# A two-block model kernel on one core: memory loaded ahead of x at the begin, and four k's of the second merge set into the stick-breaking attention

## The chip, the cores and the metric

One core of a Trainium2 chip runs one program. Its engines work side by side and meet through semaphores: TensorE (PE; its weight loads are listed as PEld), VectorE (DVE), ScalarE (ACT), GpSimd (POOL) and SyncE (SP), which issues most of the transfers. The metric is the program's time on the device in microseconds; less is better.

## The reference, cut to what matters

The model takes x (1024 positions by 1024) and a memory of 256 rows by 1024, all in float32. The first block computes

```
h   = rms_norm(x, norm_mix);  p = h @ w_in              # incl. the lora columns wd, ad, gd
x   = x + merged(rwkv7(p), conv(p)) @ w_out_mix
mem_n = rms_norm(mem, norm_mem);  k, v = split(mem_n @ w_kv)
x   = x + cross_attention(rms_norm(x, norm_xattn), k, v) @ w_xo
x   = x + relu(rms_norm(x, norm_mlp) @ w_up)^2 @ w_down
```

and the second block, on the normed result,

```
y_a = gated_delta_rule(...) @ w_up_a;   y_b = stick_breaking(q_b, k_b, v_b) * silu(z_b) @ w_up_b
out = x + (gates_a * y_a + gates_b * y_b) @ w_out
```

Stick-breaking weighs key j for query i by sigmoid(z_ij) times the product of (1 - sigmoid(z)) over the keys between j and i.

## The kernel before, in words

Every matrix product is made to float32 precision from parts: an operand is rounded to fp32r (hi), what is left is a second part (lo), and three products hi-hi, lo-hi, hi-lo are summed. So each weight tile is loaded raw, rounded (w_hi) and subtracted (w_lo) before TensorE can use it. `Weights` (L89) does this for streams of tiles with two or three slots; GpSimd rounds and subtracts in `split_tile` (L155), or ScalarE in `round_tile` and another engine in `subtract_tile`.

The program is a chain of blocks. At the end of a block all engines meet; each engine's order inside a block is written out by hand. The next block's first loads and splits are already issued inside the block (`following`).

**The begin** (`start_to_loras`, L4493). SP loads two tiles of memory and eight tiles of x (128 rows by 1024, 512 KB each), then tiles of w_kv (16 of them: eight k's for the keys, eight for the values), four raw buffers in turn. Some 25 small loads, issued by ACT (18) and SP (7), bring the vectors into rows of one buffer. TensorE turns each tile by eight transposes (`Start.turn`, L4294), DVE copies them out (L4338), TensorE turns the vectors (L4311). ACT then has the vectors and rounds memory's eight k's, scaled by norm_mem (L4330), DVE subtracts (L4352). ACT also sums the squares of all ten tiles (L4319). Then come 16 products of 12 matmuls of 512 columns (`MemoryKeys.products`, L4408): each waits for its w_kv tile's rounding on ACT (L4394) and subtraction on DVE (L4398). Beside them ACT and DVE make the norm of x: roots, factors, a spread of the factors over the partitions by TensorE (L4466), and for each k a scale on DVE (L4480), a rounding on ACT (L4485) and a subtraction on DVE (L4490). The keys are evicted after product 8 by ACT (L4417), turned by TensorE (L4425), copied (L4432) and stored. Last in the block are three lora tiles of w_in (L280), 48 matmuls each; their w_lo parts are made by DVE (L177). SP loads the next stage's weights when all of these are subtracted.

**The stick-breaking attention** (`stick_breaking`, L6165) has 48 steps: four pairs of heads (ct), eight query blocks, and one or two halves of keys. For step n TensorE computes scores (L6273, L6277), ACT the two sigmoids (L6347, L6349), DVE a running product along the keys (scan, L6403), GpSimd multiplies (L6249), TensorE transposes the weights (L6289), ACT copies them (L6365), and TensorE sums the values (L6306). TensorE's order is: scores of step n + 2, sum of step n - 1, transposes of step n. When a pair's half is summed, DVE multiplies by the gate (L6382), ACT rounds (L6353) and DVE subtracts (L6387) into the branch's hi and lo parts, k = 4 to 7 of the merge's operand; k = 0 to 3 are there from the delta rule. After the last step GpSimd splits two tiles of the merge's weights, and TensorE multiplies the first tile (eight k's of six matmuls, two groups of banks), still inside the block. The merge's own block begins behind it, and its first loads (L124) go out then.

## Time and profile before

| | us |
|---|---|
| median of 3 runs (lowest, highest) | 2924.9 (2922.48, 2925.77) |
| the profiled execution | 2924.86 |
| its span | 2923.1 |
| busy: PE, PEld | 2802.2, 2241.7 |
| busy: DVE, ACT, POOL | 1599.4, 1121.9, 1328.5 |

The span is the time from the first to the last recorded instruction of one execution. A busy time counts the stretches in which an engine has an instruction running; register, branch and semaphore instructions and the issue of transfers are not counted. The granted clock (PEclk) is a share of TensorE's full 2.4 GHz; 0.50 is 1.2 GHz. "a <- b" in brackets behind an idle time names what ended it. Instructions of one kind that follow each other closely stand in one row of a timeline with their count.

### The profile page before, as it was taken

How to read it: one execution, taken by the hardware profiler on the slowest of the kernel's cores; microseconds unless marked ns; L12 is line 12 of the kernel's file. 1: busy time of each engine (PE TensorE's matmuls, PEld its weight loads, DVE VectorE, ACT ScalarE, POOL GpSimd, SP SyncE). 2: the span in 40 equal slices, each digit the busy share in tenths (PEclk: the TensorE clock that was granted, in tenths of full speed). 3: DMA queues.
4: the chain of work that ended last, by engine and by line, in shares of the span. 5: the costliest groups of instructions: out<-in, count | busy, mean ns of one | idle time of the engine just before them, and what ended most of it. 6: DMA issues, size and time to landing. Idle time of an engine off the chain costs nothing. (4 is left out here: it accounts for less than half of the span.)

```text
span 2923.1 us, 48529 instructions
## 1 busy us (share of the span) xinstructions
PE 2802.2 (96%) x19890; PEld 2241.7 (77%) x19890; DVE 1599.4 (55%) x1909; ACT 1121.9 (38%) x1782; POOL 1328.5 (45%) x987
## 2 busy tenths in 40 slices
PE   7999788999999999999999999999999899999899
PEld 6777677778888876788888888678777778866687
DVE  5555443854465434555555554786768335357661
ACT  5433232564311123424444444433323335567410
POOL 1332213677745430347777775211221457745552
PEclk9999999999999999999999999999999999999999
DMA  5342433343171111122222233031234534421243
GB/s 203 113 159 94 129 91 85 119 134 90 44 227 46 50 51 44 37 87 87 89 92 87 95 100 109 15 111 56 88 94 136 167 93 122 127 83 63 74 136 126
DMA packets 318509, 288.93 MB, mean 99 GB/s; under 512 B 47858, under 2 KB 270249, under 8 KB 315610
## 3 DMA queue, kind: packets, MB, share of 16 engines
q1 hardware_dynamic: 318042, 285.89, 31.9%
q8 instruction: 153, 2.51, 0.4%
q14 instruction: 58, 0.48, 0.1%
q10 hardware_dynamic: 256, 0.07, 0.0%
HBM read 214.86 MB, written 70.65 MB: 98 GB/s over the span
## 5 line engine op out<-in xcount | busy, mean ns | idle before, releaser
L855 POOL TENSOR_TENSOR op_lo<-w_raw,op_hi 128x512 fp32r<-128x512 f32 x172 | 222.1, 1299 | 236.2 <-ACT op_hi L844 235.6
L280 PE MATMUL ps<-h_hi,w_hi 128*128 128x512 f32 x960 | 309.8, 404 | 3.1 <-PEq L6418 1.5
L280 PE MATMUL ps<-h_lo,w_hi 128*128 128x512 f32 x960 | 297.3, 391 | 0.0
L280 PE MATMUL ps<-h_hi,w_lo 128*128 128x512 f32 x960 | 296.2, 390 | 0.0
L161 POOL TENSOR_TENSOR w_hi<-w_raw,ones 128x1024 fp32r<-128x1024 f32 x54 | 132.2, 2448 | 287.7 <-PE ps L280 205.8
L280 PEld LDWEIGHTS ps<-h_hi,w_hi 128*128 128x128 f32 x960 | 178.6, 188 | 59.7 <-issue 24.8
L280 PEld LDWEIGHTS ps<-h_lo,w_hi 128*128 128x128 f32 x960 | 180.7, 188 | 38.6
L280 PEld LDWEIGHTS ps<-h_hi,w_lo 128*128 128x128 f32 x960 | 180.6, 188 | 38.7
L177 POOL TENSOR_TENSOR w_lo<-w_raw,w_hi 128x1024 fp32r<-128x1024 f32 x30 | 73.6, 2452 | 298.1 <-ACT w_hi L172 298.1
L164 POOL TENSOR_TENSOR w_lo<-w_raw,w_hi 128x1024 fp32r<-128x1024 f32 x54 | 146.5, 2714 | 4.2
L1784 DVE TENSOR_TENSOR x_t<-x_t,ps 128x512 f32<-128x512 f32 x144 | 96.2, 685 | 83.6 <-PE ps L910 56.8
L844 ACT CAST op_hi<-w_raw 128x512 fp32r<-128x512 f32 x167 | 102.5, 620 | 88.3 <-POOL w_raw L860 27.6
L860 POOL TENSOR_TENSOR w_raw<-w_raw 128x512 f32<-128x512 f32 x92 | 122.2, 1329 | 3.6
L280 PE MATMUL ps<-branch_hi,w_hi 128*128 128x512 f32 x384 | 119.0, 391 | 2.9 <-POOL w_lo L164 0.9
L5413 DVE RECIPROCAL p_root<-p_root 128x1024 f32<-128x1024 f32 x15 | 98.2, 6548 | 41.7 <-ACT p_root L5257 41.6
L280 PE MATMUL ps<-branch_lo,w_hi 128*128 128x512 f32 x384 | 118.3, 389 | 0.0
L280 PE MATMUL ps<-branch_hi,w_lo 128*128 128x512 f32 x384 | 118.3, 389 | 0.0
L6249 POOL TENSOR_TENSOR sb_weight<-sb_weight,sb_left 128x512 f32<-128x512 f32 (+3 forms) x96 | 84.9, 896 | 71.3 <-DVE sb_left L6403 70.7
L6403 DVE TENSOR_TENSOR_SCAN sb_left<-ps,sb_left,ones 128x512 f32<-128x512 f32 (+3 forms) x96 | 92.4, 1004 | 34.2 <-ACT ps L6349 32.6
L897 PE MATMUL ps<-h_hi,op_hi 128*128 128x512 f32 x256 | 99.8, 390 | 0.0
L897 PE MATMUL ps<-h_hi,op_lo 128*128 128x512 f32 x256 | 99.6, 389 | 0.0
L897 PE MATMUL ps<-h_lo,op_hi 128*128 128x512 f32 x256 | 99.6, 389 | 0.0
(742 smaller groups left out, 7316.1 us busy)
## 6 DMA issues: line engine op xcount, KB each, us to landing
w_raw<-in_w_in_dram SPq DMA_DIRECT2D x91, 512.0 KB, 4.8
mix_gates<-mix_sig SPq DMA_DIRECT2D x64, 256.0 KB, 2.4
w_raw<-in_w_up_dram SPq DMA_DIRECT2D x32, 512.0 KB, 4.2
w_raw<-in_w_down_dram SPq DMA_DIRECT2D x32, 512.0 KB, 3.5
kv_raw<-in_w_kv_dram SPq DMA_DIRECT2D x16, 512.0 KB, 6.0
mix_gate_b<-mix_gates SPq DMA_DIRECT2D x32, 256.0 KB, 5.2
mlp_t3h<-mlp_kept_t SPq DMA_DIRECT2D x6, 1024.0 KB, 5.0
mlp_t3l<-mlp_kept_t SPq DMA_DIRECT2D x6, 1024.0 KB, 5.0
```

Source lines behind the costliest of these rows:

```text
L161: pool.tensor_tensor(c.w_hi[:, s], c.w_raw[:, s], c.ones[:].unsqueeze(1).broadcast_to([P, KT, P]), ALU.mult).then_inc(c.w_rounded, 1)
L164: pool.tensor_tensor(c.w_lo[:, s], c.w_raw[:, s], c.w_hi[:, s].bitcast(F32), ALU.subtract).then_inc(c.w_split, 1)
L177: eng.tensor_tensor(c.w_lo[:, s], c.w_raw[:, s], c.w_hi[:, s].bitcast(F32), ALU.subtract).then_inc(c.w_split, 1)
L280: last = pe.matmul(o, w[:, s, k], a[:, k - offset, (half + h) * width:(half + h + 1) * width], start=(k == kts[0] and w is c.w_hi and a is ...
L844: act.copy(self.hi(o)[:], src).then_inc(self.rounded, 1)
L855: pool.tensor_tensor(self.lo(o)[:], src, self.hi(o)[:].bitcast(F32), ALU.subtract).then_inc(self.pooled, 1)
L860: pool.tensor_tensor(out, a, b, op).then_inc(self.pooled, 1)
L897: last = pe.matmul(out, w[:, k], a(k), start=start and k == 0 and w is w_hi and a is hi, stop=stop and k == HK - 1 and w is w_lo, skip_gro ...
L1784: dve.tensor_tensor(part, part, ps[:, down_banks[g, d][bank][side]], ALU.add).then_inc(down_free, 1)
L5413: v.mark(dve.reciprocal(root[:], root[:]))
L6249: pool.tensor_tensor(weight[:, n % 4, hd, 0:width], weight[:, n % 4, hd, 0:width], left[:, n % 2, hd, 1:width + 1], ALU.mult).then_inc(wei ...
L6403: dve.tensor_tensor_scan(l[:, hd, 0:width][:, ::-1], ps[:, 2 * (n % 2) + hd, 0:width][:, ::-1], c.ones[:, 0:1].broadcast_to([P, width]), l ...
```

## The change

It has two parts. In the begin, SP's order is: two memory tiles, two w_kv tiles, then x tiles and w_kv tiles by turns, with the vectors that ACT doesn't issue behind w_kv tile 4; the w_kv tiles 2 and 3 wait for nothing. norm_mem leaves the vectors and has a load, a transpose and a copy of its own. TensorE turns the memory tiles only, and then sets the turns of the x tiles behind the products 0 to 5, the vectors and the spread behind product 6. The x tiles turn into banks 4 to 7, products 0 to 7 use banks 0 to 3. Product j < 8 waits for memory's k = j alone. On ACT the squares and on DVE the copies stand between the w_kv tiles; the norm's scale, rounding and subtraction of k = j - 8 stand at w_kv tile j from 8 on. GpSimd makes the w_lo parts of the three lora tiles. The key store goes out behind w_kv tile 14 (before: behind tile 12). The x tiles and the turned keys lie in other places of the memory.

In the attention, GpSimd rounds the merge's first weight tile behind step 38 and subtracts it behind step 41 (of 0 to 47), and the second tile behind the last step. TensorE multiplies the first tile's k = 0, 1, 2 behind the transposes of steps 45, 46, 47 and k = 3 behind the last sum (`merge_part`); k = 4 to 7 follow as before.

```diff
-    def split_tile(self, pool, i, u):
+    def round_by_pool(self, pool, i, u):
...
-        pool.wait_ge(c.w_rounded, self.t0 + i * self.per + (u + 1))
-        pool.tensor_tensor(c.w_lo[:, s], c.w_raw[:, s], c.w_hi[:, s].bitcast(F32), ALU.subtract).then_inc(c.w_split, 1)
+
+    def split_tile(self, pool, i, u):
+        self.round_by_pool(pool, i, u)
+        self.subtract_tile(pool, i, u)
...
-    def load(self, eng, group):
+    def load(self, eng, group, first=0, last=None):
         eng.wait_ge(self.cleared, 1)
-        for dst, src in self.pieces(group):
+        for dst, src in list(self.pieces(group))[first:last]:
             eng.dma_start(dst, src).then_inc(self.loaded[group], 16)
...
+    def load(self, sp, *which):
+        for t in which:
+            sp.dma_start(self.xin[t][:], self.tiles[t]).then_inc(self.x_in[t], 16)
+
+    def load_gain(self, act):
+        act.dma_start(self.gain_rows[:], self.c.dram["norm_mem"].rearrange("a (n p) -> (a n) p", p=P)).then_inc(self.gain_loaded, 16)
...
     def turn(self, pe, t):
+        c, bank = self.c, self.banks(t)
+        pe.wait_ge(self.x_in[t], 16)
+        if t == 3:
+            pe.wait_ge(self.gain_copied, 1)
+        if t > 3:
+            pe.wait_ge(self.copied, t - 1)
+        for k in range(KT):
+            last = pe.transpose(c.ps[:, bank + k // 4, (k % 4) * P:(k % 4 + 1) * P], self.xin[t][:, k * P:(k + 1) * P], c.ident[:])
+        last.then_inc(self.turned, 1)
+
...
+    def turn_gain(self, pe):
         c = self.c
...
+        pe.wait_ge(self.gain_loaded, 16)
+        pe.transpose(c.ps[:, 6, 0:KT], self.gain_rows[:], c.ident[0:KT, 0:KT]).then_inc(self.gain_turned, 1)
+
...
+    def turn_vectors(self, pe):
         c = self.c
...
         for g in range(2):
             pe.wait_ge(self.vectors.loaded[g], self.vectors.total[g])
+        pe.wait_ge(self.copied, 10)
...
+    def take_gain(self, act):
+        act.wait_ge(self.gain_turned, 1)
+        act.copy(self.gain[:], self.c.ps[:, 6, 0:KT]).then_inc(self.gain_copied, 1)
+        act.wait_ge(self.gain_copied, 1)
+        act.wait_ge(self.copied, 2)
...
+    def round(self, act, *which):
+        for k in which:
+            act.activation(self.mem_hi[:, k], self.mem_t[:, k], ACT.Copy, scale=self.gain[:, k:k + 1]).then_inc(self.mem_rounded, 1)
...
-        if j < 2:
-            pass
-        elif j < self.RAW:
-            sp.wait_ge(self.start.turned, 2)
-            sp.wait_ge(self.start.squared, 2)
-        else:
+        if j >= self.RAW:
             sp.wait_ge(self.split, j - self.RAW + 1)
...
+        if half == 0:
+            pe.wait_ge(self.start.mem_split, k + 1)
...
-        pe.wait_ge(self.start.vec_copied, 1)
+        pe.wait_ge(self.start.copied, 10)
...
@@ -4522,19 +4531,24 @@
 
             @block.sync
             def _(sp):
-                start.load(sp)
-                for j in range(2):
-                    memory.fetch(sp, j)
+                start.load(sp, 0, 1)
+                memory.fetch(sp, 0)
+                memory.fetch(sp, 1)
+                start.load(sp, 2, 3)
+                memory.fetch(sp, 2)
+                start.load(sp, 4, 5)
+                memory.fetch(sp, 3)
+                start.load(sp, 6, 7, 8, 9)
+                memory.fetch(sp, 4)
                 start.vectors.load(sp, 1)
-                for j in range(2, 4):
-                    memory.fetch(sp, j)
+                start.vectors.load(sp, 0, 12)
+                memory.fetch(sp, 5)
                 start.store_masks(sp)
-                for j in range(4, 13):
+                for j in range(6, 15):
                     memory.fetch(sp, j)
                 sp.wait_ge(memory.keys_copied, 4)
                 sp.dma_start(c.scratch["mem_k"].rearrange("k p n -> p k n"), memory.keys[:]).then_inc(memory.keys_stored, 16)
-                for j in range(13, 16):
-                    memory.fetch(sp, j)
+                memory.fetch(sp, 15)
                 sp.wait_ge(memory.keys_turned, 4)
                 weights.load_first(sp)
                 sp.wait_ge(memory.done, 16)
@@ -4553,6 +4567,10 @@
             @block.gpsimd
             def _(pool):
                 start.pool(pool)
+                weights.subtract_tile(pool, 0, 0)
+                pool.wait_ge(memory.keys_stored, 16)
+                for u in range(1, 3):
+                    weights.subtract_tile(pool, 0, u)
                 pool.wait_ge(memory.done, 16)
                 pool.memset(plain[:, :, 0:1], 0.0).then_inc(cleared, 1)
                 pool.wait_ge(c.w_split, weights.t0 + weights.total)
@@ -4560,12 +4578,16 @@
 
             @block.tensor
             def _(pe):
-                start.pe(pe)
-                pe.wait_ge(start.mem_split, KT)
-                pe.wait_ge(start.copied, 10)
+                pe.wait_ge(c.begun, 1)
+                start.turn(pe, 0)
+                start.turn(pe, 1)
+                start.turn_gain(pe)
                 for j in range(16):
                     memory.products(pe, j)
-                    if j == 1:
+                    for t in ((2,), (3,), (4,), (5, 6), (7,), (8, 9))[j] if j < 6 else ():
+                        start.turn(pe, t)
+                    if j == 6:
+                        start.turn_vectors(pe)
                         norm.spread_row(pe)
                     if j == 7:
                         pe.wait_ge(norm.kept, 1)
@@ -4575,23 +4597,31 @@
                 for u in range(3):
                     weights.ready(pe, 0, u)
                     weights.multiply(pe, u, [c.ps[:, 2 * u], c.ps[:, 2 * u + 1]], c.h_hi, c.h_lo,
-                                     before=(lambda k: pe.wait_ge(norm.split, k + 1)) if u == 0 else None).then_inc(c.tile_done, 1)
+                                     before=(lambda k: norm.wait_split(pe, k)) if u == 0 else None).then_inc(c.tile_done, 1)
                     if u == 1:
                         pe.wait_ge(memory.values_taken, 4)
 
             @block.scalar
             def _(act):
-                start.vectors.load(act, 0)
-                start.act(act)
+                start.load_gain(act)
+                start.vectors.load(act, 0, 0, 12)
                 memory.round(act, 0)
+                start.take_gain(act)
+                start.round(act, 0, 1)
                 memory.round(act, 1)
+                start.round(act, 2, 3, 4, 5, 6, 7)
+                memory.round(act, 2)
+                for j in range(3, 8):
+                    for t in range(2 * (j - 3), 2 * (j - 2)):
+                        start.square(act, t)
+                    memory.round(act, j)
                 norm.root(act)
-                memory.round(act, 2)
-                memory.round(act, 3)
+                memory.round(act, 8)
+                start.take_vectors(act)
                 norm.keep_row(act)
-                for j in range(4, 16):
+                for j in range(9, 16):
                     memory.round(act, j)
-                    if j == 10:
+                    if j == 9:
                         act.wait_ge(norm.made, 1)
                         act.wait_ge(memory.done, 8)
                         for n in range(4):
@@ -4599,14 +4629,12 @@
                     if j == 12:
                         for n in range(4):
                             memory.copy_keys(act, n)
-                    if j % 2:
-                        norm.round(act, (j - 5) // 2)
+                    norm.round(act, j - 9)
                 weights.round_tile(act, 0, 0)
-                norm.round(act, 6)
+                norm.round(act, 7)
                 act.wait_ge(memory.done, 16)
                 for n in range(4):
                     memory.take(act, 1, n, factor)
-                norm.round(act, 7)
                 for u in range(1, 3):
                     weights.round_tile(act, 0, u)
                 for u in range(2):
@@ -4621,26 +4649,26 @@
 
             @block.vector
             def _(dve):
-                start.dve(dve)
+                start.copy(dve, 0)
+                start.copy(dve, 1)
                 memory.subtract(dve, 0)
+                start.subtract(dve, 0, 1)
                 memory.subtract(dve, 1)
+                start.subtract(dve, 2, 3, 4, 5, 6, 7)
+                start.copy(dve, 2)
+                memory.subtract(dve, 2)
+                start.copy(dve, 3)
+                for j in range(3, 8):
+                    memory.subtract(dve, j)
+                    for t in ((4,), (5, 6), (7,), (8, 9), ())[j - 3]:
+                        start.copy(dve, t)
                 norm.factors(dve)
-                memory.subtract(dve, 2)
-                memory.subtract(dve, 3)
-                for j in range(4, 16):
+                for j in range(8, 16):
                     memory.subtract(dve, j)
-                    if j % 2 == 0:
-                        norm.scale(dve, (j - 4) // 2)
-                    else:
-                        norm.subtract(dve, (j - 5) // 2)
-                    if j == 13:
-                        dve.wait_ge(memory.keys_stored, 16)
-                weights.subtract_tile(dve, 0, 0)
-                for k in range(6, 8):
-                    norm.scale(dve, k)
-                    norm.subtract(dve, k)
-                for u in range(1, 3):
-                    weights.subtract_tile(dve, 0, u)
+                    norm.scale(dve, j - 8)
+                    if j > 8:
+                        norm.subtract(dve, j - 9)
+                norm.subtract(dve, 7)
                 v = c.v_steps
                 dve.wait_ge(cleared, 1)
                 for u in range(2):
@@ -6248,7 +6276,12 @@
                     pool.wait_ge(scanned, 2 * n + hd + 1)
                     pool.tensor_tensor(weight[:, n % 4, hd, 0:width], weight[:, n % 4, hd, 0:width],
                                        left[:, n % 2, hd, 1:width + 1], ALU.mult).then_inc(weighted, 1)
-            following.split_some(pool, 2)
+                if n == n_steps - 10:
+                    following.round_by_pool(pool, 0, 0)
+                if n == n_steps - 7:
+                    following.subtract_tile(pool, 0, 0)
+            following.split_tile(pool, 0, 1)
+            following.ahead = 2
 
         @block.tensor
         def _(pe):
@@ -6307,6 +6340,17 @@
                                          weight_t[:, n % 2, hd, t * P:(t + 1) * P], start=n in begins and t == 0,
                                          stop=n in ends and t == 3, skip_group_check=True)
                 last.then_inc(summed, 1)
+
+            def merge_part(k):
+
+                if k == 0:
+                    following.ready(pe, 0, 0)
+                    pe.wait_ge(scanned, 2 * (n_steps - 1))
+                s = following.slot(0)
+                for w, a in ((c.w_hi, c.br_hi), (c.w_hi, c.br_lo), (c.w_lo, c.br_hi)):
+                    for h in range(2):
+                        pe.matmul(ps[:, h], w[:, s, k], a[:, k, h * HALF:(h + 1) * HALF], start=k == 0 and w is c.w_hi and a is c.br_hi,
+                                  stop=k == CT - 1 and w is c.w_lo, skip_group_check=True)
 
             for h in range(2):
                 turn_values(0, h)
@@ -6322,15 +6366,18 @@
                 ct, at_step = divmod(n, per)
                 if at_step in early and ct + 1 < CT:
                     turn_values(ct + 1, early.index(at_step))
+                if n >= n_steps - 3:
+                    merge_part(n - n_steps + 3)
             sum_values(n_steps - 1)
+            merge_part(3)
 
             def before(k):
                 for h in range(2) if k >= CT else ():
                     pe.wait_ge(split[h], k - CT + 1)
 
             pe.wait_ge(scanned, 2 * n_steps)
-            following.multiply_early(pe, [([ps[:, 0], ps[:, 1]], range(CT)), ([ps[:, 2], ps[:, 3]], range(CT, KT))],
-                                     c.br_hi, c.br_lo, before)
+            following.early = True
+            following.multiply(pe, 0, [ps[:, 2], ps[:, 3]], c.br_hi, c.br_lo, kts=range(CT, KT), before=before).then_inc(c.tile_done, 1)
 
         @block.scalar
         def _(act):
```

## Rows read from the trace of the kernel before

**Rows 1.** The page's part 1: busy us (share of the span) xinstructions.

```profile
PE 2802.2 (96%) x19890; PEld 2241.7 (77%) x19890; DVE 1599.4 (55%) x1909; ACT 1121.9 (38%) x1782; POOL 1328.5 (45%) x987
```

**Rows 2.** Timeline, begin: start us, us, engine, line, out<-in xcount [idle before <-releaser].

```profile
4.66 6.54 PE L4299 MATMUL ps<-ident,x_in 128*128 128x128 f32 x32 [4.66 <-DMA x_in<-in_mem_dram]
...
8.34 1.23 DVE L4338 COPY mem_t<-ps 128x1024 f32<-128x1024 f32 x1 [0.48 <-PE ps L4299]
...
21.22 0.66 PE L4311 MATMUL ps<-ident,vec_rows 128*128 128x128 f32 x2 [5.07 <-DMA vec_rows<-in_sb_k_gain_dram]
...
21.67 3.14 PE L4299 MATMUL ps<-ident,x_in 128*128 128x128 f32 x16
...
30.04 1.19 PE L4408 MATMUL ps<-kv_hi,mem_hi 128*128 128x512 f32 x2 [5.23 <-DVE kv_lo L4398]
...
81.98 0.62 PE L280 MATMUL ps<-h_hi,w_hi 128*128 128x512 f32 x2
```

**Rows 3.** Windows: us, busy PE, PEld, DVE, ACT, POOL; PEclk, DMA, GB/s.

```profile
4.66:10.00 5.34, 5.34 (x25) 5.20 (x26) 2.45 (x2) 1.77 (x2) 4.56 (x13) 1.00 1.01 394
...
27.00:30.00 3.00, 0.00 (x0) 0.00 (x0) 2.78 (x5) 2.98 (x5) 0.00 (x0) 0.60 0.01 3
...
30.00:34.00 4.00, 3.96 (x9) 3.13 (x10) 3.61 (x4) 2.12 (x3) 0.00 (x0) 0.50 0.69 197
...
50.00:60.00 10.00, 10.00 (x45) 8.28 (x45) 8.47 (x8) 7.08 (x9) 0.00 (x0) 1.00 0.35 118
...
70.00:74.00 4.00, 1.57 (x7) 1.01 (x6) 1.59 (x2) 2.41 (x3) 0.00 (x0) 1.00 0.99 341
```

**Rows 4.** Waits of PE, 2730 to 2753 us: total, times, longest.

```profile
PE ps L6306 <- ACT sb_weight_t L6365: 3.4, 3, 1.2
```

**Rows 5.** Timeline of the attention's end and the merge's begin.

```profile
2709.95 3.39 POOL L6249 TENSOR_TENSOR sb_weight<-sb_weight,sb_left 128x512 f32<-128x512 f32 x4 [2.04 <-DVE sb_left L6403]
...
2718.45 1.24 POOL L6249 TENSOR_TENSOR sb_weight<-sb_weight,sb_left 128x256 f32<-128x256 f32 x2 [0.36 <-DVE sb_left L6403]
...
2719.05 0.66 DVE L6399 COPY sb_left<-sb_left 128x2 f32<-128x2 f32 x1
...
2722.31 0.65 PE L6289 MATMUL ps<-ident,sb_weight 128*128 128x128 f32 x4
...
2741.85 0.70 PE L280 MATMUL ps<-branch_hi,w_hi 128*128 128x512 f32 x2 [0.88 <-POOL w_lo L164]
...
2742.39 2.23 DVE L6387 TENSOR_TENSOR branch_lo<-sb_o,branch_hi 128x512 fp32r<-128x512 f32 x1 [0.69 <-ACT branch_hi L6353]
...
2753.33 0.71 PE L280 MATMUL ps<-branch_hi,w_hi 128*128 128x512 f32 x2 [0.32 <-PEq L6213]
```

**Rows 6.** Groups by line, 0 to 90 us: busy us, mean ns | idle.

```profile
L4398 DVE TENSOR_TENSOR kv_lo<-kv_raw,kv_hi 128x1024 fp32r<-128x1024 f32 x16 | 19.5, 1222 | 16.2 <-ACT kv_hi L4394 16.2
...
L4394 ACT CAST kv_hi<-kv_raw 128x1024 fp32r<-128x1024 f32 x16 | 16.7, 1051 | 16.3 <-PE ps L4408 8.8 <-DMA kv_raw<-in_w_kv_dram 7.5
...
L4480 DVE SCALAR_TENSOR_TENSOR mix_whole<-x_t,vec,mix_row 128x1024 f32<-128x1024 f32 x8 | 10.2, 1279 | 0.0
...
L4490 DVE TENSOR_TENSOR h_lo<-mix_whole,h_hi 128x1024 fp32r<-128x1024 f32 x8 | 9.8, 1222 | 2.2 <-ACT h_hi L4485 2.2
...
L4352 DVE SCALAR_TENSOR_TENSOR mem_lo<-mem_t,vec,mem_hi 128x256 fp32r<-128x256 f32 x8 | 3.4, 481 | 5.5 <-ACT mem_hi L4330 5.5
...
L4417 ACT ACTIVATE w_raw<-ps,square_sums 128x512 f32<-128x512 f32 x4 | 2.4, 689 | 0.0
...
L4466 PE MATMUL ps<-mix_diag,ones 128*128 128x512 f32 x4 | 1.9, 591 | 0.0
```

**Rows 7.** The page's part 5, GpSimd subtracting weights: busy us, mean ns.

```profile
L164 POOL TENSOR_TENSOR w_lo<-w_raw,w_hi 128x1024 fp32r<-128x1024 f32 x54 | 146.5, 2714 | 4.2
```

**Rows 8.** Timeline, the next stage's weights: SP's issue and GpSimd's first use.

```profile
90.02 2.21 SPq L126 DMA_DIRECT2D w_raw<-in_w_in_dram  x3
...
94.16 2.39 POOL L161 TENSOR_TENSOR w_hi<-w_raw,ones 128x1024 fp32r<-128x1024 f32 x1 [11.85 <-DMA w_raw<-in_w_in_dram]
```

More of the change, by code:

```diff
@@ L4249, in __init__ @@
         self.vec_turned, self.vec_copied = c.sem("vec_turned"), c.sem("vec_copied")
+        self.gain_loaded, self.gain_turned, self.gain_copied = (c.sem(f"mem_gain_{n}") for n in ("loaded", "turned", "copied"))
         self.mem_rounded, self.mem_split = c.sem("mem_rounded"), c.sem("mem_split")
@@ L4318, in square @@
         wait(act, self.squared, t - 1)
[L4319 to L4332 removed]
+        act.activation(self.junk[t % 2][:], self.xin[t][:], ACT.Square, accum_out=self.sums[:, t:t + 1]).then_inc(self.squared, 1)
@@ L4477, in scale @@
             dve.wait_ge(self.kept, 1)
+            dve.wait_ge(self.start.vec_copied, 1)
         if k > 1:
-            dve.wait_ge(self.split, k - 1)
+            self.wait_split(dve, k - 2)
         dve.scalar_tensor_tensor(out=self.whole[k % 2][:], in0=c.x[:, k], scalar=vec(c, "norm_mix", k), in1=self.row[:],
```

70 lines of the change are left out of this document (22 added, 48 removed).

## The prediction

> **What bounds the kernel now.** I read the page's busy shares first: TensorE (PE) is busy for 2802.2 of 2923.1 us [rows 1]. An engine that is this full can only be helped where it stands idle or runs slowly, so next I went through the timeline for those stretches. In the begin the first transpose starts at 4.66 us, memory's second tile is copied by 9.57, PE stands 5.07 us for the last vector's load and turns the vectors at 21.22, the first of the 16 memory products starts at 30.04, and the first lora product at 81.98 [rows 2]. So 25 us pass between the first transpose and the first product. The windows add the clock: 1.2 GHz (granted 0.50) in 30 to 34 us, after PE had idled for the 3 us before; then 2.4 GHz, with 45 matmuls in the 10 us from 50 on [rows 3], some 0.225 each, so a product of 12 matmuls is 2.7 us (I use 2.72). Sixteen are 43.5 us; the begin spends 51.9 on them and what lies between. The second place is the end of the stick-breaking attention, a relay of PE transposes, ScalarE's copy (ACT) and PE sums, in which PE waits 3.4 us in three places [rows 4], and then 0.88 us for the weights [rows 5].
>
> **Part 1, the begin: what goes and what comes.** Nothing is taken off PE; the same products, transposes and spreads are laid in another order. What goes is the wait of memory's rows for all vectors and for the x tiles. I set up a ledger, each engine in its new order, most durations from [rows 6].
>
> Start. The two memory tiles load first, as before, so copy 1 still ends at 9.57 [rows 2]. The stretch 4.66 to 10 moves 394 GB/s [rows 3], so a 512 KB tile lands each 1.33 us: w_kv tile 0 near 7.3, tile 1 near 8.6, the last x tile near 22, w_kv 4 near 23. ACT has rounded tile 0 (1.05) and waits for copy 1; VectorE (DVE) then subtracts tile 0 (1.22, to 10.8) and the first memory k (0.43, to 11.2). Product 0 starts at 11.2 instead of 30.04.
>
> Clock. PE has idled from 8.4 to 11.2 by then. The row of 27 to 30 shows the clock falling (mean 0.60) in an idle of that size, that of 70 to 74 shows 1.00 kept with PE busy for 1.57 of 4 us [rows 3], so product 0 costs between 2.7 us (2.4 GHz) and 5.2 us (1.2 GHz). I take 4.1, in the middle: its end is 15.3.
>
> Products 1 to 6, with eight x tiles turned between them: 6 x 2.72 = 16.3, and 8 x 0.95 = 7.6 (between 0.8 and 1.57: the last two took 3.14 together, behind an idle of 5.07 us [rows 2], and I take the fast end with some gap to the next). PE has no wait in this stretch: DVE has one subtraction and at most two copies (1.22 + 2 x 1.23 = 3.7) beside 3.7 to 4.6 of PE, ACT a rounding and two squares. End of product 6: 39.2. Now DVE is late: the last copy follows the last turn (36.5) behind the copy before it, to 38.1; subtraction 7 to 39.3, the norm's factors (a small instruction and one of the copy's size, 1.5) to 40.8. The spread takes 1.9 [rows 6], to 42.7. Here a new wait stands in PE's order (product 7 behind the spread): it costs 1.6 us, the turn of the vectors in it. Product 7 runs to 45.5.
>
> Products 8 to 15 are bound by DVE, not PE: each has a subtraction 1.22, a scale 1.28 and a norm subtraction 1.22 [rows 6] = 3.72, against 2.72 on PE. DVE has scale 0, subtraction 9 and scale 1 behind it at 47.6; then it waits for ACT, which must first evict the keys (2.4 [rows 6], from 45.5) and round (1.05): 49.1. From there six norm subtractions and six w_kv subtractions (12 x 1.22 = 14.6) and five scales (6.4) lead to w_kv 15's: 70.1. Its product ends at 72.8. The turning of the keys hides in PE's slack here.
>
> Lora weights. ScalarE rounds weight tile 0 near 69; POOL now subtracts it in place of DVE, 2.71 each on the page [rows 7] against 1.22, to about 72; beside DVE's last subtractions it may be later, so I add 0.2. **Lora start 73.0 against 81.98: -9.0 us.** Its last norm parts come at 73.4, and k = 7 needs them only at 82.5. Tiles 1 and 2 are rounded behind the four evictions (2.4) and two roundings, and POOL is done with them near 81.3, 8.3 us behind the lora start; PE wants tile 1 at 83.9. Before, SP issued the next stage's loads at 90.02, 8.0 behind the start, and POOL took them up at 94.16 [rows 8]. The same distance, so that all later stages move forward as a block. The other queues: SP now has w_kv 4 wait for subtraction 0 with the vectors, w_kv 5 and the masks behind it; PE needs the vectors at 39, they land near 24. ACT issues 13 small loads instead of 18. The mem_k store goes out behind w_kv 14; before it stood ahead of w_kv 13, and PE was busy for only 1.57 of the 4 us from 70 on [rows 3]. Only w_kv 15 is behind it now, due near 65, landing near 64.
>
> Bounds of this part: the clock up at once (-1.4) and the turns at 0.85 instead of 0.95 (-0.8) give a lora start of 70.8; slow for all of product 0 (+1.1) and the turn behind it (+0.6), and 0.1 us more at each of thirteen handoffs, 76.0. So -6.0 to -11.2.
>
> **Part 2, the merge's first four k.** It adds no matmul: four k of six (4 x 1.36 = 5.4 us) move ahead of the block's end. Three (4.1) stand in the three gaps of 3.4 in all [rows 4], 0.7 more than these. The fourth follows the last sum, where before 0.88 was waited for w_lo [rows 5]. So the block ends earlier by 5.44 + 0.88 - 0.7 - 1.36 = 4.3. The last branch rest, due at k = 7, is there: DVE makes it some 3 us behind the last sum, k = 7 comes 5.4 behind it. The merge's block opens when PE is through (2753.33, on the block's release [rows 5]); its loads go out then, so all of it follows.
>
> Price: POOL rounds tile 0 behind step 38 and subtracts behind step 41, about 2.4 and 2.7 in gaps of 2.04 and 0.36 [rows 5]. The first pushes POOL 0.3; I take nothing for so little. The second pushes step 42's product 2.3; PE's transposes of it, at 2722.31, stand 2.6 behind its old end (2719.69): just enough. DVE's two-element copy at 2719.05 lasts 0.66, until POOL's running instruction ends; so does a subtraction of 2.23 beside POOL's rounding at 2742.39 [rows 5]. With the long subtraction there, that copy lasts to about 2720.7 and the scan behind it starts 0.3 late. I take 0.3; both POOL instructions exposed in full would be 5.1, the bound on the other side. **Part 2: -4.0, from -4.6 to +0.8.**
>
> A rule weighed against it: the Trainium skill, page SBUF — State Buffer, section Who interferes with whom, says that VectorE and GpSimd share a port pair as an exclusive lock held for the whole instruction. The trace agrees (0.66 and 2.23 us above). By it alone DVE's copy would wait for the end of POOL's subtraction, which is the 0.3 already taken.
>
> **Sum.** -9.0 - 4.0 = -13.0 on the profiled execution's 2924.86, which lies 0.04 under the median of the three runs (2924.9): 2911.9 us, written as 2912.
>
> **The rivals.**
> The clock stays low longer: product 1 and its turns at 1.2 GHz too. For it: from 30.04 to 34 PE ran matmuls and stayed at 1.2 GHz [rows 3]. Against it: behind product 0 PE has no idle in which the level would stay down. Product 1 and its turn cost 2.4 + 0.6 more, and nothing behind absorbs it: 2915.
> POOL's inserts are exposed in the attention: the margin at step 42 is only 0.3 us, and steps 43 to 47 are one relay. Part 2 falls to about 0: 2916.
> The lora weights come late, since POOL does in 2.7 what DVE did in 1.22: lora tile 1 or the next stage's weights 3 to 4 us late: 2916.
> The load order does not do what it says: if transfers of the queue were served together rather than in order, the first product would wait for x tiles too, near 19. Against it: the first tile had landed by 4.66 with others issued behind it [rows 2]. Then -9 shrinks to -2: 2919.
> Slower: PE never reaches 2.4 GHz in the products, because each now waits for a piece from DVE. A product is 5.16 then, 2.43 more; from six such products on, all of the 13 us is spent. With all sixteen, and turns, spread and keys at half speed (104 us of work from 11.2), the lora starts at 115.5: 2924.9 + 33.5 - 4 = 2954. Against it: 70 to 74 us kept 1.00 at a PE busy for 1.57 of 4 us.
>
> **How the numbers follow.** Forecast 0.70; clock longer 0.12; POOL exposed 0.07; late weights 0.03; load order 0.03; never fast 0.03; else 0.02. What a measurement here can tell from no change is about 0.2%, 5.9 us, so the line is 2919. All but the last rivals are under it; of the load order I give half to no change. Faster 0.93, within 0.2% 0.03, slower 0.04. The likeliest case has -9.0 (-6 to -11.2) and -4.0 (-2.5 to -4.6): 2909 to 2916.5. The range takes in the exposed POOL and late weights with the best and the worst of part 1, but for their far corner: 2907 to 2919.
>
> **What would show each step.** First product near 11.2, its matmuls at 1.2 or 2.4 GHz. No PE wait over 0.5 us until product 6; one of about 1.6 before the spread; waits near 1 us on DVE's kv_lo in products 12 to 15. Lora start 73, next stage's first load 8.3 behind. Attention: merge matmuls after the transposes of steps 45 to 47, POOL's subtraction near 2718 less 9, the block's end 13 us earlier than before. The prediction is wrong if products 8 to 15 aren't paced by DVE (faster than 3.7 each), if the lora start moves without the end following, or if the attention's steps lengthen by over 1 us.

## The result, and the profile after

| | median us | runs | ratio to before, 95% interval |
|---|---|---|---|
| before | 2925.77 (2922.48 to 2931.11) | 5 | |
| the changed kernel | 2906.47 (2899.85 to 2909.45) | 5 | 0.9933 [0.9922, 0.9944] |
| forecast | 2912.0, range 2907 to 2919 | | 0.9956 of the three runs then known |

The kernel became 0.67% faster, in the direction forecast, and landed 0.5 us below the low end of the range: the prediction missed on the size. The profiled execution after took 2909.33 us against 2924.86.

PE's busy time and the whole span, after ([rows 1] before):

```profile
span 2907.6 us, 48536 instructions
## 1 busy us (share of the span) xinstructions
PE 2800.9 (96%) x19891; PEld 2240.2 (77%) x19891; DVE 1589.8 (55%) x1906; ACT 1121.8 (39%) x1783; POOL 1336.8 (46%) x990
```

PE's busy time is 1.3 us less (2802.2 before); the other 14.2 of the 15.5 us by which the span is shorter went from its idle time. The begin on the timeline after (start us, us, engine, line, out<-in, count, idle before and its releaser):

```profile
10.90 1.18 PE L4412 MATMUL ps<-kv_hi,mem_hi 128*128 128x512 f32 x2 [2.82 <-DVE mem_lo L4359]
...
12.73 1.05 PE L4412 MATMUL ps<-kv_lo,mem_hi 128*128 128x512 f32 x2
...
14.39 0.62 PE L4412 MATMUL ps<-kv_hi,mem_lo 128*128 128x512 f32 x2
...
15.30 1.03 PE L4314 MATMUL ps<-ident,x_in 128*128 128x128 f32 x8
...
40.37 1.95 PE L4474 MATMUL ps<-mix_diag,ones 128*128 128x512 f32 x4 [1.15 <-issue]
...
48.58 1.23 DVE L4499 TENSOR_TENSOR h_lo<-mix_whole,h_hi 128x1024 fp32r<-128x1024 f32 x1 [1.56 <-ACT h_hi L4494]
...
57.93 0.74 PE L4412 MATMUL ps<-kv_hi,mem_hi 128*128 128x512 f32 x2 [0.20 <-DVE kv_lo L4400]
...
64.72 1.28 DVE L4489 SCALAR_TENSOR_TENSOR mix_whole<-x_t,vec,mix_row 128x1024 f32<-128x1024 f32 x1
64.86 0.74 PE L4412 MATMUL ps<-kv_hi,mem_hi 128*128 128x512 f32 x2 [0.41 <-DVE kv_lo L4400]
...
65.92 1.22 DVE L4499 TENSOR_TENSOR h_lo<-mix_whole,h_hi 128x1024 fp32r<-128x1024 f32 x1
...
67.06 1.22 DVE L4400 TENSOR_TENSOR kv_lo<-kv_raw,kv_hi 128x1024 fp32r<-128x1024 f32 x1
...
68.12 2.40 POOL L179 TENSOR_TENSOR w_lo<-w_raw,w_hi 128x1024 fp32r<-128x1024 f32 x1 [51.02 <-ACT w_hi L174]
68.19 3.42 DVE L4489 SCALAR_TENSOR_TENSOR mix_whole<-x_t,vec,mix_row 128x1024 f32<-128x1024 f32 x1
68.33 0.74 PE L4412 MATMUL ps<-kv_hi,mem_hi 128*128 128x512 f32 x2 [0.41 <-DVE kv_lo L4400]
...
71.23 0.61 PE L282 MATMUL ps<-h_hi,w_hi 128*128 128x512 f32 x2
```

The first product stands at 10.90 (30.04 in [rows 2]). Two matmuls take 1.05 us at first and 0.62 later: 1.2 GHz, then 2.4 GHz inside product 0, which takes 4.4 with what stands between it and the turn. Read the starts on DVE: 64.72, 65.92, 67.06, 68.19. From scale to scale, three instructions, it is 3.47 us, while their durations add to 3.72: each starts before the last one's duration is over. DVE works without a pause from 48.58 to the lora and paces the products at 3.47, but PE feels it only from product 12 (57.93) on; products 8 to 11 run at PE's own pace, with the turn of the keys between them. The lora starts at 71.23 (81.98 in [rows 2]): -10.8.

Every first product of the following stages up to 290 us stands 10.7 or 10.8 us earlier too, and the attention begins 10.6 earlier (2580.3, now 2569.7). Its end, after, answers to [rows 4, 5]:

```profile
2706.80 2.35 POOL L179 TENSOR_TENSOR w_lo<-w_raw,w_hi 128x1024 fp32r<-128x1024 f32 x1
2707.80 1.38 DVE L6446 COPY sb_left<-sb_left 128x2 f32<-128x2 f32 x1
...
2719.94 1.09 PE L6322 MATMUL ps<-ident,sb_weight 128*128 128x128 f32 x8
2721.07 0.70 PE L6352 MATMUL ps<-branch_hi,w_hi 128*128 128x512 f32 x2
...
2724.49 0.70 PE L6352 MATMUL ps<-branch_hi,w_hi 128*128 128x512 f32 x2
...
2727.92 0.71 PE L6352 MATMUL ps<-branch_hi,w_hi 128*128 128x512 f32 x2
...
2729.49 1.09 PE L6339 MATMUL ps<-sb_weight_t,sb_v_nat 128*64 128x128 f32 x16
2730.52 0.73 PE L6352 MATMUL ps<-branch_hi,w_hi 128*128 128x512 f32 x2
...
2732.01 0.62 PE L282 MATMUL ps<-branch_hi,w_hi 128*128 128x512 f32 x2
...
2737.93 0.70 PE L282 MATMUL ps<-branch_hi,w_hi 128*128 128x512 f32 x2 [0.32 <-PEq L6241]
```

The three gaps and the 0.88 for w_lo are gone; the block's end moved from 2753.33 to 2737.93, -15.4, of which 10.6 was there at the attention's begin and 11.2 at step 45's turn (2731.13 before, 2719.94 after); the other 4.2 lie behind it. From step 45's turn to the last sum PE takes 9.55 us (2719.94 to 2729.49); before it was 8.75 (2731.13 to 2739.88). The 0.8 between them is about the 0.7 by which three k's (4.1) are longer than three gaps (3.4). DVE's small copy beside POOL's subtraction took 1.38, until that subtraction ended, as forecast, but no step came later for it: DVE's next scan stands at 2709.22, 11.2 earlier than before (2720.40), like the transposes around it. POOL's subtraction took 2.35 here, not the 2.7 of the forecast.

### The profile page after: what moved, and what is told of

Its sections match the earlier page's. It is cut to its first block and busy times, and to the rows that moved or that the text cites. A ratio compares the mean times of both kernels' runs of the same rounds, so it can differ in the third digit from the quotient of the medians.

```text
span 2907.6 us, 48536 instructions
## 1 busy us (share of the span) xinstructions
PE 2800.9 (96%) x19891; PEld 2240.2 (77%) x19891; DVE 1589.8 (55%) x1906; ACT 1121.8 (39%) x1783; POOL 1336.8 (46%) x990
## 5 line engine op out<-in xcount | busy, mean ns | idle before, releaser
L179 POOL TENSOR_TENSOR w_lo<-w_raw,w_hi 128x1024 fp32r<-128x1024 f32 x87 | 226.1, 2599 | 359.0 <-ACT w_hi L174 354.8
L899 PE MATMUL ps<-h_hi,op_lo 128*128 128x512 f32 x256 | 99.6, 389 | 0.0
L899 PE MATMUL ps<-h_lo,op_hi 128*128 128x512 f32 x256 | 99.6, 389 | 0.0
L862 POOL TENSOR_TENSOR op_sum<-w_raw 128x512 f32<-128x512 f32 x56 | 72.4, 1293 | 57.7 <-PE ps L912 33.0
```

The source lines that it names most:

```text
L179: eng.tensor_tensor(c.w_lo[:, s], c.w_raw[:, s], c.w_hi[:, s].bitcast(F32), ALU.subtract).then_inc(c.w_split, 1)
L862: pool.tensor_tensor(out, a, b, op).then_inc(self.pooled, 1)
L899: last = pe.matmul(out, w[:, k], a(k), start=start and k == 0 and w is w_hi and a is hi, stop=stop and k == HK - 1 and w is w_lo, skip_gro ...
```

## The experiments

I had two theories of the 5.5 us between forecast and median. A: each of the two places is worth what its stage shows, somewhat more than I took, and the rest is chance of the executions. B: something systematic lies beyond the two places.

**e1, e2: each part alone; e3: the changed kernel again.** Five rounds each, in one sitting.

```diff
 e1: the changed kernel without the attention's part
-                if n >= n_steps - 3:
-                    merge_part(n - n_steps + 3)
             sum_values(n_steps - 1)
-            merge_part(3)
 e2: the kernel before, and the same lines with POOL's two added
+                if n == n_steps - 10:
+                    following.round_by_pool(pool, 0, 0)
+                if n == n_steps - 7:
+                    following.subtract_tile(pool, 0, 0)
```

> The begin's half of the change alone. Theory A (two places, each worth what its own stage shows; the rest of the median's distance is the chance of when TensorE's clock stands low): lora start at 71.2 us, every later stage 10.8 us earlier than before except where the clock differs, attention's end and last stage no earlier than that; total -10.8 us, within 3 us for the clock. Theory B (the begin moves something further along as well, such as which stretches run at the low clock): total -14 us or more, with a stage between 290 and 1000 us that is shorter in this run too.

> The merge's four k's within the attention, alone. Theory A: nothing before 2585 us moves; the merge's last rows come 4.9 us earlier; total -4.9 us, within 3 us for the clock. Theory B (the gain there was partly an accident of where the begin had put it): the end moves by 4 us or less or by more than 6. My prediction's term was -4.0.

> The whole change once more. Theory A: the sum of the two parts, 15.7 us under before in the mean, with runs that lie up to 10 us apart; those with the higher mean granted clock are the faster ones, by about the difference of clocks times the span (0.001 is 2.9 us). Theory B: the median is again 19 us under before whatever the clock of the runs is.

| | median us | ratio to before [95%] | lora start |
|---|---|---|---|
| before | 2922.27 (17 runs) | | 81.98 |
| e1, begin only | 2909.1 (6) | 0.9959 [0.9945, 0.9973] | 72.7 |
| e2, attention only | 2918.2 (12) | 0.9987 [0.9978, 0.9995] | 81.5 |
| e3, both | 2904.14 (6) | 0.9938 [0.9923, 0.9952] | 72.3 |

The parts add: 0.9959 x 0.9987 = 0.9946, inside e3's interval. Each is real, and no interplay shows beyond the noise. e1's own profile warns how much chance is in one execution: its rwkv scan starts 9.2 us earlier than before and its attention 15.4 earlier (2564.9), although the code between them is the same. Theory B's sign, a shorter stage between 290 and 1000 us, is there (6.3 us from the scan's start to L334), but e2, with the old begin, has it too (3.6), so it is no sign of the new begin. Lora starts of one and the same begin differ by more than a microsecond (71.2 after, 72.3, 72.7), because product 0 took 4.4 us once, 5.3 in e1 and 5.2 in e3 (two matmuls at 1.05 us almost to its end). That is the upper end of the range that I had given this product.

**e4: the norm's subtractions on POOL.** Is it DVE's number of instructions that counts, or who else works beside it?

```diff
 pool:
+                for k in range(8):
+                    norm.subtract(pool, k)
 dve:
-                    if j > 8:
-                        norm.subtract(dve, j - 9)
-                norm.subtract(dve, 7)
```

> The change, with the eight norm subtractions of the begin on GpSimd in place of VectorE, which paced products 12 to 15 at 3.47 us each. If the pace is VectorE's instruction count alone: it falls to 2.4 us a tile, TensorE becomes the bound at 2.72, the lora start comes 2 to 3 us earlier (68 to 69). If VectorE's two-input instructions stand while GpSimd's subtraction (2.4 us) runs: 2.4 + 2.4 = 4.8 us a tile, lora start 8 to 10 us later (79 to 81).

One run: 2920.5 us, lora start 82.7. The timeline of e4:

```profile
65.57 6.76 POOL L4499 TENSOR_TENSOR h_lo<-mix_whole,h_hi 128x1024 fp32r<-128x1024 f32 x2 [2.24 <-ACT h_hi L4494]
...
66.67 3.41 DVE L4400 TENSOR_TENSOR kv_lo<-kv_raw,kv_hi 128x1024 fp32r<-128x1024 f32 x1
...
70.14 0.74 PE L4412 MATMUL ps<-kv_hi,mem_hi 128*128 128x512 f32 x2 [1.51 <-DVE kv_lo L4400]
...
74.60 0.73 PE L4412 MATMUL ps<-kv_hi,mem_hi 128*128 128x512 f32 x2 [1.45 <-DVE kv_lo L4400]
...
80.26 7.03 POOL L179 TENSOR_TENSOR w_lo<-w_raw,w_hi 128x1024 fp32r<-128x1024 f32 x3
...
82.70 1.19 PE L282 MATMUL ps<-h_hi,w_hi 128*128 128x512 f32 x2 [5.09 <-issue]
```

Eight instructions less on DVE, and the begin is 11.5 us longer than after, later than either branch of the expectation. Two things make it. First the pace: beside a POOL subtraction a DVE instruction of 1.22 takes 3.41, as the scale at 68.19 did after. What was moved to POOL costs DVE 2.2 us of POOL's 2.4 a time, more than the 1.22 that it took off. PE waits 1.4 to 1.5 us for DVE's kv_lo at each product from 11 on, the products start 4.5 us apart in place of 3.47, and product 15 starts at 74.60 in place of 68.33: 6.3 us. Second the lora's weights: in POOL's own order their subtraction now stands behind the norm's last two. It starts at 80.26 (68.12 after), and PE idles 5.09 us for it; its first two matmuls after that take 1.19.

**e5 and e9: DVE's order in the tail.** PE idles some 0.75 us for each of products 12 to 15. Does it need more than another order? e5 moves the norm's instructions behind the w_kv subtractions where the two buffers of the norm allow it. The lists give the new orders in words.

```diff
 e5, dve:                          e9, dve:
+ w_kv 12, scale 4, w_kv 13,      + w_kv 12, scale 4, w_kv 13, norm 3,
+ norm 3, w_kv 14, scale 5,       + scale 5, w_kv 14, norm 4, w_kv 15,
+ w_kv 15, norm 4, scale 6, ...   + scale 6, norm 5, scale 7, norm 6, 7
                                   e9, act:
-                    norm.round(act, j - 9)
+                    if j < 15:
+                        norm.round(act, j - 9)
                 weights.round_tile(act, 0, 0)
+                norm.round(act, 6)
```

> The changed kernel with VectorE's order at products 12 to 15 laid anew: subtraction 12, scale 4, subtraction 13, norm subtraction 3, subtraction 14, scale 5, subtraction 15, and the norm's remaining scales and subtractions behind it, so that three of them no longer stand ahead of the last products' pieces. Theory A (VectorE paces the tail of the products, at 3.47 us a tile, and TensorE's 2.72 is what is left without it): the waits of 0.2 to 0.41 us on kv_lo at products 12 to 15 go, the products end at 69.2 to 70.0 us instead of about 71.2, and the lora starts at 69.5 to 70.3, 1 to 2 us earlier; the norm's parts, now about 2 us later in VectorE's order, are still ahead of the lora's need. Theory B (the tail is paced by the weights' landing or by TensorE itself): the lora start stays within 0.4 us of 71.2 to 72.7, where the runs of this begin put it.

> The changed kernel with a second new order for the tail of the begin, which takes ScalarE's order in as the first one didn't: VectorE does subtraction 12, scale 4, subtraction 13, norm subtraction 3, scale 5, subtraction 14, norm subtraction 4, subtraction 15, and only then scales 6 and 7 with the rest of the norm; ScalarE rounds the lora's first weight tile ahead of the norm's part 6. Theory A (VectorE's place in the order paces products 12 to 15 at 3.47 us; the first new order failed because ScalarE's rounding of the weights stood behind a scale that had been moved back, so that the lora waited 4.1 us): the products run at 2.7 to 2.9 us each behind product 12, they end 57.5 to 58.6 us behind the first product's start (60.3 in the changed kernel), and the lora starts there, 69.0 to 70.0 us in all, 1.5 to 2.5 us earlier; the end follows it, 2902 to 2905 us by median. Theory B (the weights' landing and GpSimd's subtraction of them set the lora start): the products end earlier, but the lora start stays within 0.5 us of 60.3 behind the first product.

e5 (one run, 2913.13 us) missed its aim: lora start 75.6. Its timeline:

```profile
67.17 1.22 DVE L4400 TENSOR_TENSOR kv_lo<-kv_raw,kv_hi 128x1024 fp32r<-128x1024 f32 x1 [2.06 <-ACT kv_hi L4396]
...
70.89 1.05 ACT L4494 CAST h_hi<-mix_whole 128x1024 fp32r<-128x1024 f32 x1 [3.75 <-DVE mix_whole L4489]
71.84 1.04 ACT L174 CAST w_hi<-w_raw 128x1024 fp32r<-128x1024 f32 x1
...
75.61 1.19 PE L282 MATMUL ps<-h_hi,w_hi 128*128 128x512 f32 x2 [4.10 <-issue]
```

ScalarE's order still had the norm's roundings ahead of w_kv 15's and of the lora's weights; with the scales moved back on DVE, ACT idled 3.75 us and PE 4.10, after which even the clock was down (1.19 for two matmuls). The queue beside the one I changed decided. e9 takes ACT's order in. PE's products 12 and 14 now start at 59.56 and 65.48, 2.96 apiece against 3.47: DVE's order did pace the tail. And yet the lora starts at 72.36 and not at 69 to 70, behind a new wait:

```profile
67.62 1.28 DVE L4489 SCALAR_TENSOR_TENSOR mix_whole<-x_t,vec,mix_row 128x1024 f32<-128x1024 f32 x1
67.74 4.52 POOL L179 TENSOR_TENSOR w_lo<-w_raw,w_hi 128x1024 fp32r<-128x1024 f32 x1 [50.93 <-ACT w_hi L174]
...
72.36 0.70 PE L282 MATMUL ps<-h_hi,w_hi 128*128 128x512 f32 x2 [1.15 <-issue]
```

POOL's subtraction, due at 70.1 with its 2.40, ends at 72.26: begun 0.12 us behind a scale of DVE's, it waited for that one and the next. From product 12's start the lora is 12.8 us away (13.3 after). Median 2904.14 (6 runs), ratio 0.9933 [0.9917, 0.9948].

**e6 and e10: keeping PE awake before product 0.**

```diff
                 start.turn_gain(pe)
+                for n in range(20):
+                    pe.transpose(c.ps[:, 7, (n % 4) * P:(n % 4 + 1) * P], start.xin[1][:, 0:P], c.ident[:])
```

> The changed kernel with 20 more transposes of memory's second tile, into a bank that nobody reads yet, in TensorE's idle ahead of product 0. If the clock of product 0 (0.43 us a matmul at first, 4.2 us for the product) is low because TensorE idled from 8.4 to 10.9 us, it keeps or finds 2.4 GHz: product 0 takes 2.7 to 3.6 us and the lora starts 0.6 to 1.5 us earlier. If the level is set by something else, say the time since the kernel's start, product 0 stays at 4.0 to 4.3 us and the lora start moves by less than 0.3 us. By both, the first product itself starts within 0.2 us of 10.9 to 11.3, since it waits for VectorE's piece.

> The order of e9 and the 20 transposes of e6 ahead of product 0 together. Both touch other parts of the same chain of products, so they should add: product 0 at 2.8 us instead of 4.2 (1.4 us, of which 0.5 was lost to a later first product in e6 and 0.5 more to VectorE, which paces the tail), the tail at 2.7 to 2.9 a product. Lora start 68.3 to 69.6 us; median 2900 to 2905 us. If the gain of the clock is not passed on, because VectorE's chain behind the spread sets the pace and starts from the spread, the lora start is that of e9 within 0.3 us.

The timeline of e6:

```profile
8.39 3.25 PE L4586 MATMUL ps<-ident,x_in 128*128 128x128 f32 x20
11.39 0.71 PE L4412 MATMUL ps<-kv_hi,mem_hi 128*128 128x512 f32 x2
...
13.78 0.62 PE L4412 MATMUL ps<-kv_lo,mem_hi 128*128 128x512 f32 x2
14.24 1.04 PE L4314 MATMUL ps<-ident,x_in 128*128 128x128 f32 x8
```

Product 0 took 2.85 us, 2.82 in e10 and 2.84 in e12; in the eight profiles of this begin without the added transposes it took 4.3 to 5.3. So it is the idle of 2.8 us in front that takes the clock down. The gain arrives in part: lora start 70.8 in e6 (one run, 2909.04 us) and 70.3 in e10 (median 2904.41, ratio 0.993 [0.9916, 0.9945]). e10 still waited 1.15 for POOL, as e9 did, and so missed the 68.3 to 69.6 that I expected.

**e7 and e12: who makes the lora's weights.** e7 puts the three subtractions back on DVE; e12 is e10 with only the first on DVE, right behind w_kv 15's.

```diff
 e12, pool:
-                weights.subtract_tile(pool, 0, 0)
 e12, dve:
                 memory.subtract(dve, 15)
+                weights.subtract_tile(dve, 0, 0)
```

> The changed kernel with the subtractions of the first three lora weight tiles back on VectorE, as before the change, instead of GpSimd. Theory A (GpSimd's subtraction of 2.4 us holds VectorE's last scale, 3.42 us for 1.28, so moving it costs VectorE as much as it saves): the last scale is back at 1.3 us, VectorE has 1.2 us more of its own and 2.1 us less of the hold, and the lora starts within 0.8 us of 71.2 to 72.7. Theory B (the relief of VectorE by GpSimd is a real part of the gain): the lora starts 1.2 us or more later, at 73.5 or beyond.

> The kernel of e10 with the subtraction of the lora's first weight tile on VectorE, right behind subtraction 15, instead of GpSimd. In e9 and e10 GpSimd's subtraction began 0.1 to 0.2 us behind a scale of VectorE's and took 4.45 to 4.52 us where 2.40 is its time, and the lora start waited 1.15 us for it. If this contention alone holds the lora back behind the new order, VectorE makes the tile in 1.2 us (by 67 us), the lora starts with the end of product 15, 11.4 to 11.7 us behind the start of product 12 (12.8 in e9 and e10, 13.3 in the changed kernel), 68.7 to 69.5 us in all, and the median is 1.0 to 1.3 us under e10's, 2901 to 2905 us. If the weights' landing sets it (ScalarE waited 0.27 to 0.35 us for it), the lora starts no earlier than 69.8.

e7 (one run, 2907.05 us): lora start 71.91, 0.7 later than after and inside the scatter of that begin; PE waits 0.49 in front of it. POOL's relief of DVE, a part of the change, is worth nothing to 0.7. e12's timeline:

```profile
64.04 1.05 ACT L174 CAST w_hi<-w_raw 128x1024 fp32r<-128x1024 f32 x1 [0.26 <-DMA w_raw<-in_w_in_dram]
65.12 1.23 DVE L179 TENSOR_TENSOR w_lo<-w_raw,w_hi 128x1024 fp32r<-128x1024 f32 x1
...
68.55 0.62 PE L282 MATMUL ps<-h_hi,w_hi 128*128 128x512 f32 x2
```

1.23 us in place of 4.52, and PE goes from the last product into the lora without a wait, at 68.55: 11.5 behind product 12, as expected of the contention. Median 2902.3 (2900.97 to 2908.17, 6 runs), ratio 0.9924 [0.9912, 0.9936], the lowest of all kernels here. Its stage is 2.7 us shorter than after, by three changes together: the order, the transposes, and the subtraction, which alone took the way from product 12 to the lora from 12.8 us in e10 to 11.5. By medians the intervals of e12 and of the changed kernel overlap.

**e8 and e11: the same code again.** e8 is the kernel before, unchanged; e11 the changed one, in five more rounds.

> The kernel before, unchanged, profiled once more. Theory A (what lies between the stage shifts and the medians is when TensorE's clock stands low, which differs from execution to execution of the same code): the stretch from the start of the rwkv scan to its first output product, 201.1 us in the first profile of it, differs by 1 us or more, with the low-clock time of the profile differing in the same direction, while the begin's marks (first product 30.0, lora start 82.0) and the long middle stage (1279.9 us) stay within 0.5 us. Theory B (the kernel before has a fixed pace and only the changed one is faster later on): that stretch is within 0.3 us of 201.1.

> The changed kernel once more, timed on the chip and against the runs of before that the two kernels beside it have. Theory A (each place is worth what its stage shows, 9.7 to 10.8 and 4.9 to 5.3 us, and what the medians show beyond that is the rwkv scan's opening, whose length differs with the clock): ratio 0.994 to 0.9955, and the scan's opening of this profile, from its first transposes to L2600's first matmul, 27.5 us if the clock is up in its second 10 us, 30 us or more if it is low there. Theory B (a systematic gain beyond the two places): ratio 0.9925 to 0.9938.

e8 (2924.31 us; another run of before beside it took 2931.93) has its begin's marks within 0.5 us of the first profile (first product 29.6, lora 82.2) and its long middle stage within 0.2, but the rwkv scan's opening, from its first matmul to the first of L2600, took 31.5 us in place of 27.3. The three 10 us windows from the scan's start, before:

```profile
300.80:310.80 10.00, 6.53 (x144) 5.82 (x146) 3.78 (x8) 0.80 (x2) 4.29 (x6) 0.50 0.53 151
310.80:320.80 10.00, 6.86 (x212) 5.64 (x207) 4.95 (x10) 2.83 (x5) 4.02 (x5) 0.99 0.57 144
320.80:330.80 10.00, 7.80 (x316) 6.82 (x317) 4.78 (x12) 2.62 (x5) 1.59 (x2) 1.00 0.41 104
```

and in e8 (PE busy first, PEclk third from the end):

```profile
301.00:311.00 10.00, 6.45 (x148) 5.72 (x148) 3.78 (x8) 0.84 (x2) 4.29 (x6) 0.54 0.51 145
311.00:321.00 10.00, 5.96 (x158) 4.75 (x156) 3.13 (x6) 1.76 (x3) 4.01 (x5) 0.84 0.61 149
321.00:331.00 10.00, 7.19 (x188) 6.16 (x191) 5.41 (x13) 2.34 (x4) 0.00 (x0) 0.77 0.19 44
```

The clock is up by the second window in one, and down again in the third in the other: 158 and 188 matmuls in place of 212 and 316. The profile of the changed kernel happened to have the slow opening (31.5 us, 0.50, 0.84, 0.76), e3 a quick one (27.7), e11 one between (29.2, where I had expected 27.5 or 30 and more). Behind the opening part of it comes back, so that the whole scan stage took 201.1, 202.9 and 199.0 us in the three profiles with the old begin (before, e8, e2) and 197.6 to 203.0, mean 200.4, in the eleven with the new. Not all of that follows the clock: e1 was low for longer than before (0.72 and 0.83 in its second and third window), and its stage was the shorter one (197.7). From the scan's first matmul to the attention's, where the code is the same in all, the three took 2277.1 to 2279.5 us (mean 2278.7) and the eleven 2273.4 to 2282.0 (mean 2278.0).

e11: 2909.41 us (6 runs) against 2925.37 (11 runs), ratio 0.9948 [0.9935, 0.9961]. That is inside theory A's range (0.994 to 0.9955), where the first comparison and e3 had B's (0.9925 to 0.9938).

## Why the prediction was right, and where it failed

**What bounds it, and the direction: right.** Both places gave time, and the gain of the begin was carried to the end, stage by stage. None of the five rivals came; product 1 ran at 0.70 or 0.71 us for its first two matmuls in every profile of this begin, POOL's inserts hid, the lora's weights were in time. The next stage's loads did go out later than forecast (80.87, 9.6 behind the lora start and not 8.3), since POOL ends its third subtraction only at 80.84, but the stages behind are 10.7 us earlier all the same. (In the slow rival 11.2 + 104 is 115.2, not 115.5; nothing rests on it.)

**First product (forecast 11.2): right**, 10.90 and 11.0 to 11.4 in the other profiles without added transposes. **Product 0 (4.1, between 2.7 and 5.2): inside its bounds after** (4.4), and up to 5.3 in others. The 4.1 was a middle between the two levels and no mechanism; that 4.4 fell near it is luck. **Spread: right**: forecast at 40.8, seen at 40.37 (39.5 to 42.0 in the others), behind a wait of 1.15 where I had 1.6 with the turn of the vectors (0.4) in it.

**The pace of products 8 to 15: the step that was mis-sized.** "each has a subtraction 1.22, a scale 1.28 and a norm subtraction 1.22 [rows 6] = 3.72". DVE was the bound, but it took 3.47: I had added durations where starts are nearer together. The sign that I had set for this step, "faster than 3.7 each", was met: right in the cause, wrong in the size. From 49.1 the forecast had 21.0 us of such work; by 3.47 / 3.72 it is 19.6, and the trace has 19.7, from 48.58 to 68.28. Product 15 ended at 71.2 in place of 72.8: 1.3 from the pace and 0.5 from the chain's earlier begin, less 0.2 since the last product took 2.9. With the 0.2 that I had added for POOL's subtraction and that was not needed, this is where -9.0 became -10.8. Over the four profiles of this begin (71.2, 71.5, 72.3, 72.7: mean 71.9, against 81.9 over three of the old) it is -10.0. The waits on kv_lo are 0.2 to 0.41 at products 12 to 15, not near 1. e9 confirmed the cause: another order on DVE made the same products 2.96 apart.

**The attention (-4.3 by steps, +0.3, so -4.0): right by steps.** From step 45's turn to the next stage's first matmul at L623, eleven profiles with the part took 94.2 to 95.3 us (mean 94.8), three without 98.9 to 99.6 (mean 99.4): -4.6. The 0.3 for the held copy did not come, since POOL's subtraction took 2.35 us and not 2.7 and so let the copy end just in time for the scan; from the attention's first matmul to step 45's turn it is 149.7 to 150.8 us without the part and 147.9 to 151.0 with it. The Trainium skill, page SBUF — State Buffer, section Who interferes with whom, has VectorE and GpSimd take their port pair as a lock for a whole instruction; e4's 3.41 and e9's 4.52 us agree with it, in both directions, though in e9 GpSimd waited for two VectorE instructions that follow each other closely, not for one. I used the rule for a copy of two elements and not for the 1 us instructions of the begin, where it cost VectorE 2.1 us a time.

**The sum, and the range: the second thing that failed.** By stages the two places are worth 9.97 + 4.56 = 14.5 us where 13.0 stood: 1.5 of the 5.5 us. The two profiled executions, 15.5 us apart, fit this: 10.7 from the begin, 0.4 between, 4.4 from step 45's turn on. The rest of the 5.5 us is not in a step. The distance of the medians was 19.3, 18.1 and 16.0 us in three sittings, and runs of one and the same kernel lie 4 to 14 us apart, with the scan's opening alone different by up to 4 before part of it comes back. My range took the median as exact and had no term for the scatter: the best case of the steps (-11.2 and -4.6) gives 2909.1, and the 2 us from there down to 2907 have no reason in the prediction. The spread of the three sittings is some 2 us on either side of its middle; with 2 us more, 2906.47 is inside, but this is said with the result known. Whether some of the 1.5 to 4.8 us beyond the stages is systematic stays open. Against it: over the long stretch of the same code, from the scan to the attention, the means with and without the new begin differ by only 0.7 us while single profiles differ by 8.6, and the intervals of e3 (14.0 to 22.5 us) and e11 (11.4 to 19.0 us) hold 14.5. For it: the first comparison's (16.4 to 22.8) does not.

## What to carry to other kernels

Pace an engine by the distance of its starts in a row of such instructions, not by the sum of their durations. When one engine's order is changed, write down the orders of the engines that hand to it, and who runs beside it: here first ScalarE's order and then GpSimd's shared time with VectorE ate what a new order had won (lora start 75.6, then 72.4, and 68.6 with POOL's subtraction moved and the transposes of e6 added). And before a range is given for a gain of half a per cent, look how far runs of the unchanged kernel lie apart, and add it.

## What the runs showed of the hardware

- A 128x1024 VectorE instruction with another right behind it starts 1.13 to 1.20 us after the last, with durations of 1.22 to 1.28.
- VectorE and GpSimd hold each other up: VectorE's 1.22 or 1.28 becomes 3.4 beside one 2.4 us GpSimd instruction, and GpSimd's own 2.40 became 4.45 to 4.52 when it began 0.1 to 0.2 us behind one of VectorE's.
- PE, idle for 2.7 to 3.0 us, came back at 1.2 GHz for most of a product in seven of eight profiles, and stayed there until 14 to 17 us; in e11 it began at 2.4 GHz (0.70 us for two matmuls) and fell to 1.2 (1.06) only 1.5 us into the product. With transposes in most of the idle it was at 2.4 from the first matmul, three times of three.
- The PEclk column can miss this: it reads 0.50 from 11 to 14 us after, but 1.00 from 11 to 17 us in e1, e3, e5 and e9, where two matmuls took the same 1.05 us. Durations of matmuls are the surer sign.
